# A two-layer decoder trunk: GpSimd sums of the down operand blocks, and down results placed in PSUM ahead of the tail's products

## What is computed

```python
h = rms_norm(x, ffn_pre_g[l])
f = jax.nn.silu(jnp.einsum('bsd,df->bsf', h, w_gate[l])) * jnp.einsum('bsd,df->bsf', h, w_up[l])
f = jnp.einsum('bsf,fd->bsd', f, w_down[l])
x = x + rms_norm(f, ffn_post_g[l])
# next layer
h = rms_norm(x, attn_pre_g[l]); u = h @ w_in[l]   # then four mixers, w_out, norm, residual
```

## Time and profile before

| | |
|---|---|
| three runs | 1068.89, 1071.06, 1071.44 us, median 1071.06 |
| the profiled execution | 1069.37 us, of which its span is 1067.6 |
| TensorE busy | 1028.0 us, 96% |
| VectorE busy | 896.6 us, 84% |
| ScalarE busy | 539.7 us, 51% |
| GpSimd busy | 65.2 us, 6% |
| mean granted TensorE clock | 0.993 |

### The profile page before, as it was taken

One profiled execution on the slowest core, in us unless ns is written; L12 is line 12 of the kernel. 1 busy time (PEld: TensorE's weight loads), 2 busy tenths in 40 slices (PEclk: granted clock), 3 DMA queues, 4 the chain that ended last, 5 costly groups with the idle time before them and its releaser, 6 DMA issues.

```text
span 1067.6 us, 21327 instructions
## 1 busy us (share of the span) xinstructions
PE 1028.0 (96%) x8470; PEld 832.6 (78%) x8470; DVE 896.6 (84%) x1788; ACT 539.7 (51%) x968; POOL 65.2 (6%) x86
## 2 busy tenths in 40 slices
PE   8999999999999998999988999999999999989996
PEld 5888895597888887888477888847878888878872
DVE  6999988985889899778699888988758989997657
ACT  5645454653666665426254363455446666654231
POOL 1000000010111110000000000000011111100000
PEclk9999999999999999999998999999999999999998
DMA  9512321363678863526034131224447777634212
GB/s 339 194 61 87 112 67 53 100 149 79 173 173 206 206 179 102 168 80 225 12 108 130 61 118 61 80 80 121 89 114 174 194 203 180 182 121 121 79 60 79
DMA packets 72883, 136.69 MB, mean 128 GB/s; under 512 B 8656, under 2 KB 8912, under 8 KB 72656
## 3 DMA queue, kind: packets, MB, share of 16 engines
q1 hardware_dynamic: 62992, 117.50, 33.6%
q0 software_dynamic: 9792, 17.83, 10.8%
HBM read 133.20 MB, written 2.10 MB: 127 GB/s over the span
## 4 chain that ended last, share of the span: by engine, by line
PE 72%; DVE 16%; issue 5%; ACT 4%; SPq 1%; DMA 1%; DVEq 0%; ACTq 0%
PE ps L696 31%; PE ps L804 17%; PE ps L873 14%; DVE ring L1660 4%; PE ps L700 3%; PE ps L894 2%; PE ps L1025 1%; DVE R L2029 1%; PE ps L1009 1%; ACT ring L1095 1%; DVE gbc L2047 1%; DMA raw<-weights_dram 1%; DVE ps L2105 1%; DVE E L1774 1%; SPq L617 1%
## 5 line engine op out<-in xcount | busy, mean ns | idle before, releaser
L1660 DVE SCALAR_TENSOR_TENSOR ring<-raw,ring 128x512 f16<-128x512 f32 (+2 forms) x368 | 320.3, 901 | 61.4 <-ACT ring L1095 61.3
L1095 ACT ACTIVATE ring<-raw 128x512 f16<-128x512 f32 (+2 forms) x368 | 278.0, 796 | 137.0 <-DVE raw L1630 59.9
L696 PE MATMUL ps<-hT,ring 128*128 128x256 f16 (+1 forms) x1632 | 195.5, 279 | 0.0
L696 PEld LDWEIGHTS ps<-hT,ring 128*128 128x128 f16 x1632 | 159.4, 98 | 28.8
L804 PE MATMUL ps<-E,ring 128*128 128x256 f16 x1224 | 145.3, 273 | 10.5 <-ACT gt L1095 9.7
L804 PE MATMUL ps<-hT,ring 128*128 128x256 f16 x1224 | 145.4, 273 | 0.0
L804 PEld LDWEIGHTS ps<-E,ring 128*128 128x128 f16 x1224 | 118.1, 98 | 29.5 <-ACT gt L1095 14.7
L696 PE MATMUL ps<-ring,hT 128*128 128x256 f16 x1152 | 134.6, 274 | 3.6 <-DVE hT L1782 3.5
L804 PEld LDWEIGHTS ps<-hT,ring 128*128 128x128 f16 x1224 | 119.8, 98 | 13.8
L696 PEld LDWEIGHTS ps<-ring,hT 128*128 128x128 f16 x1152 | 112.7, 99 | 19.5 <-issue 4.4
L1822 DVE SCALAR_TENSOR_TENSOR E<-E,par 128x256 f32<-128x256 f32 x240 | 102.0, 476 | 0.2
(11 more groups left out here) (172 smaller groups left out, 1148.3 us busy)
## 6 DMA issues: line engine op xcount, KB each, us to landing
raw<-weights_dram SPq DMA_DIRECT2D x402, 256.0 KB, 3.5
raw<-weights_dram POOLq DMA_DIRECT2D x68, 256.0 KB, 5.1
gbc<-gains_dram SPq DMA_DIRECT2D x8, 512.0 KB, 5.6
xs<-x_dram SPq DMA_DIRECT2D x4, 512.0 KB, 6.5
U<-weights_dram SPq DMA_DIRECT2D x8, 256.0 KB, 7.4
out_dram<-xs SPq DMA_DIRECT2D x8, 256.0 KB, 2.0
cst<-consts_dram SPq DMA_DIRECT2D x1, 1296.0 KB, 11.9
bd<-pool_w_dram SPq DMA_DIRECT2D x8, 16.0 KB, 9.7
```

Source lines behind the costliest of these rows:

```text
L696: ins = mm(dst, st, mv_, start=first and i == 0, stop=last and i == 2, **kw)
L1095: return A(dst, src, ACT.Copy, scale=scale)
L1660: V.scalar_tensor_tensor(out=at[1], in0=src, scalar=W_SCALE, in1=at[0], op0=ALU.mult, op1=ALU.subtract).then_inc(lo_split, 1)
```

## The change

1. `fS_sums` moves to GpSimd, as four instructions with no scalar_tensor_tensor among them. In GpSimd's queue it stands ahead of the accumulating DMAs of block 2p+5 (the last one behind those of block 21).
2. On ScalarE the hi halves of these sums (`fS_hi`) stand behind both shared results' copies, `u_copy` and `v_copy`, and ahead of weight chunks 2 and 3; on VectorE `fS_lo` stands behind `c22_add`. The order of chunks in the units f = 20 and 21 is changed too.
3. For tiles 1 to 3 `yq` is put into the tile's banks ahead of its tail products, which accumulate on it: `y0_copy` on ScalarE and `y1_sum` on VectorE. Only tile 0 keeps `y_sum`. `square_y` of tiles 1 to 3 waits for the unit alone. Two matmuls for each layer are added in `dn_seven`, which write half banks that ScalarE then overwrites.
4. Around the step to the second layer the splits of slots 2, 3 and 4 and the squares, norms and halves are put in another order, and three numbers of AT change.

```diff
-        ("pre_T", 2): 39, ("pre_T", 3): 63, ("moba_T", 0): 65, ("moba_T", 1): 82, ("moba_stage", 0): 106,
+        ("pre_T", 2): 33, ("pre_T", 3): 56, ("moba_T", 0): 70, ("moba_T", 1): 82, ("moba_stage", 0): 106,
...
+            def fS_sums(l, p):
+                i = 4 * (fS_no(l, p) - 1)
+                pool.wait_ge(f_sb, fno(l, 2 * p + 1, 0))
+                if i:
+                    pool.wait_ge(s_lo, 2 * (fS_no(l, p) - 1))
+                nc.gpsimd.tensor_tensor(f_sum[:, 0:2 * HALF].rearrange("p (c t) -> p c t", c=2),
+                                f_all[:, HALF:3 * HALF].rearrange("p (c t) -> p c t", c=2),
+                                f_all[:, 3 * HALF:4 * HALF].unsqueeze(1).to_broadcast([P, 2, HALF]),
+                                ALU.subtract).then_inc(s_sum, 1)
+                nc.gpsimd.tensor_tensor(f_sum[:, 2 * HALF:3 * HALF], f_all[:, 3 * HALF:4 * HALF], f_all[:, HALF:2 * HALF],
+                                ALU.subtract).then_inc(s_sum, 1)
+                pool.wait_ge(s_sum, i + 2)
+                nc.gpsimd.tensor_tensor(f_sum[:, 2 * HALF:3 * HALF], f_sum[:, 2 * HALF:3 * HALF], f_all[:, 2 * HALF:3 * HALF],
+                                ALU.subtract).then_inc(s_sum, 1)
+                pool.wait_ge(s_sum, i + 3)
+                nc.gpsimd.tensor_tensor(f_sum[:, 3 * HALF:4 * HALF], f_sum[:, 2 * HALF:3 * HALF], f_all[:, 0:HALF],
+                                ALU.add).then_inc(s_sum, 1)
             for i, n in enumerate(FAST_SLOTS):
+                l, f = n // SLOTS, n % SLOTS - GU0
+                for p in DN_FAST:
+                    if f == 2 * p + 5:
+                        fS_sums(l, p)
...
+                        if first and g and blk == 6:
+                            mm(bank[banks[t]][:, half(1)], a[0][:, tok(t)], dn_blocks(n, j, 0, blk, blk + 1),
+                               start=False, stop=True, skip_group_check=True)
...
-                fresh = tail0 and p == PLAIN[0]
+                fresh = tail0 and p == PLAIN[0] and t == 0
+                if k == TAIL0 and t:
+                    pe.wait_ge(y1_in, (NT - 1) * l + t)
+                    pe.wait_ge(y0_in, 5 * l + 2 * t - 1)
...
+            def y0_copy(l, t):
+                act.wait_ge(q_sb, 6 * (2 * l + 2))
+                copy(bank[PAIR[t]][:, :], yq[t][:, 0:512]).then_inc(y0_in, 1)
+                if t > 1:
+                    act.wait_ge(y1_in, (NT - 1) * l + t)
+                    copy(bank[PAIR[t] + 1][:, half(1)], yq[t][:, 512 + HALF:DM]).then_inc(y0_in, 1)
...
+            def y1_sum(l, t):
+                dve.wait_ge(q_sb, 6 * (2 * l + 2))
+                cols = slice(0, 512 if t == 1 else HALF)
+                b = bank[PAIR[t] + 1][:, cols]
+                V.tensor_tensor(b, b, yq[t][:, 512:DM][:, cols], ALU.add).then_inc(y1_in, 1)
```

More of the change, by code:

```diff
@@ L1347, in main_steps @@
                     due = fp % 2 and in_seven(fp)
-                    if not due:
+                    late = due or f >= FT - 2
+                    if not late:
                         split_hi_chunks(new, 1, 2)
                     hidden_hi(l, *HIDDEN[i - 1])
+                    if f in FAST:
+                        u_copy(l, f)
+                    if late:
+                        split_hi_chunks(new, 1, 2)
+                    else:
+                        split_hi_chunks(new, 2, 3)
+                    if f in FAST:
+                        v_copy(l, f)
                     if due:
                         fS_hi(l, fp // 2)
[L1353 to L1359, removed]
+                    if f == FT - 1:
+                        break
+                    if late:
+                        split_hi_chunks(new, 2, 3)
                     split_hi_chunks(new, 3, 4)
                 silu(l, *HIDDEN[i1 - 1])
+                split_hi_chunks(FREED_BY[l * NU + FIRST_OF[GU0] + i1 - 2], 2, 4)
                 split_hi(*FREED_BY[l * NU + FIRST_OF[GU0] + i1 - 1])
@@ L1637, in split_lo_part, with lo_part @@
                     dn_weight_sums(slot, part // 2)
+                lo_part(slot, part)
+            def lo_part(slot, part):
+                n = PARTS * slot + part
                 if fast(slot) and part == 1:
@@ L1736, in norm_y @@
                 r = rstd(t, (y_sq, n + 1))
+                if between:
+                    between()
                 if t == 0:
@@ L2129, in main_steps @@
                     due = fp % 2 and in_seven(fp)
-                    if due:
-                        fS_sums(l, fp // 2)
-                    else:
+                    if not due and not down:
                         split_lo_chunks(new, 1, 2)
@@ L2136, in main_steps @@
                         c12_add(l, f)
+                    if down:
+                        for part in range(2):
+                            lo_part(new[0], part)
+                        if f == FT - 2:
+                            dn_weight_sums(new[0], 1)
+                            c22_add(l, f)
+                            fS_lo(l, fp // 2)
+                            for part in range(2, PARTS):
+                                lo_part(new[0], part)
+                        else:
+                            c22_add(l, f)
+                        continue
                     if due:
-                        fS_lo(l, fp // 2)
                         split_lo_chunks(new, 1, 2)
```

133 lines of the change are left out of this document (74 added, 59 removed).

## The result

| | before | after |
|---|---|---|
| median, us (range, 4 runs each) | 1069.97 (1068.24 to 1071.44) | 1080.96 (1079.33 to 1082.50) |
| span of the profiled execution | 1067.6 | 1079.3 |
| gate and up stage of a layer | 163.10 | 172.01, 171.99 |
| seven-product down stage of a layer | 78.54 | 78.76, 78.75 |
| from the first layer's tail to the second's gate and up stage | 286.04 | 282.41 |

The changed kernel is slower: ratio 1.0103, interval 1.008 to 1.0127. The stage lengths are differences of TensorE's rows at the stages' borders, such as 425.29 in the earlier trace rows and 1031.51 in the earlier trace rows.

A forecast was written before the change was run, and what follows sets the result against it. TensorE, busy for 96% of the span, was taken as the bound, so only its waits, half clock and end could give time. +6.3 - 4.9 - 6.7 - 2.2 + 0.4 = -7.1 us gave 1064 us, range 1047 to 1083.

The forecast's parts named there:

- Rival A: Gate and up: GpSimd's sums end late beside VectorE's SBUF reads, +1.4 us a pair, +20 us, 1084 us; chance 0.27.
- units 20 and 21: Last two gate and up units: they lose 0.8 us instead of 3.24, -4.9 us for two layers.
- the step: Step into the second layer: shorter waits and no half clock, partly lost at the first attention stages; -6.7 us.
- Even unit: Gate and up: `u_copy` no longer waits for the sums, so the 0.57 us lost in an even unit are gone.
- Odd unit: Gate and up: hidden comes late, the unit takes 10.19 us, the pair 19.36 against 18.91; +6.3 us over 14 pairs.
- GpSimd's sums: Gate and up: four instructions of 1280 columns in all, taken at 3.5 us, between 1.8 and 5.2.
- the cover of 0.8: Gate and up: sums end at 391.0, ScalarE asks at 391.8; each further us costs 14 us for the kernel.
- no half clock: Step into the second layer: TensorE would not run at half clock there, where it had cost 2.0 us less 1.6.
- End and added matmuls: After TensorE's last matmul the last square starts earlier, -2.2 us; four added matmuls of 256 columns cost 0.44 us.
- GpSimd's queue: Accumulating DMAs of slot 21 start behind the sums but stay hidden, unless the sums end after 393.3.
- Rival B: Gate and up: no wait moves and both units of a pair are free, 14.3 us less, 1048 us; chance 0.25.

The follow-up runs named there:

- E1: The changed kernel with the sums of the down operand blocks made by VectorE again, in three instructions behind hidden; 1066.54 us, ratio 0.9966.
- E3: The changed kernel with ScalarE's `fS_hi` moved behind chunk 2 of the weights in even units, GpSimd still making the sums; 1056.68 us, ratio 0.9874.
- E6: The changed kernel with GpSimd's first sum made twice in each pair; 1107.95 us, ratio 1.0361.
- E4: The kernel before with only the sums moved to GpSimd, `fS_hi` still ahead of `u_copy`; 1120.95 us, ratio 1.0471.
- E8: E2 with 96 GpSimd instructions that nobody waits for (adds and memsets) put into layer 1; 1075.78 us, ratio 1.0051.
- E5: The changed kernel with the edits of E1 and E3 together: sums on VectorE, halves behind chunk 2; 1052.46 us, ratio 0.9830.
- E2: The kernel before, with its gate and up loop and sums kept, plus the new tail, step and end; 1061.47 us, ratio 0.9922.
- E7: E3 with ScalarE's copy of the first attention transposes moved ahead of the eighth weight block's splits; 1057.51 us, ratio 0.9882.
- E9: E5 with E7's edit, and 13 of VectorE's 18 convolution taps moved behind the fourth attention maximum; 1055.42 us, ratio 0.9865.
- E10: The kernel before with only ScalarE's `fS_hi` moved behind `v_copy`; 1106.14 us, ratio 1.0338.

## Why the prediction was wrong

I forecast 1064 and got 1081: Rival A, priced at 1084, instead of the forecast. Rival A is right in its mechanism; that its number is so near is in part luck. Its own terms (391.0 and 2.6 us) give 393.6 and not the 393.2 that I wrote, so 1.8 us a pair and some 1089, and it left the other terms as forecast. The pair lost only 0.94 us by GpSimd; units 20 and 21 and the step, both too good in the forecast, made up for it. By steps, on the profile's scale:

- **Even unit: right.** 9.17 us, no wait, as walked.
- **Odd unit, apart from GpSimd: right.** The walk gave 19.36 us for a pair with the sums on time; E1, where they are on time (because VectorE makes them), shows 19.35, with waits of 0.45 and 0.21 us in the places forecast.
- **GpSimd's sums: the step that failed.** I took 3.5 us, and they take 5.2, past the cover of 0.8. The prediction priced that end at 0.9 us a pair; the rows show 0.94. Its 12.6 us would have made the sum +5.5; the rest to the measured +11.7 is 3.1 in units 20 and 21, 3.1 at the step, and small terms. E1, E3 and E6 show it from three sides: sums on time, the queue behind them freed, and the dose. What went wrong inside the step: 3.5 us was a good price for the four alone (0.72 us for 256 columns in E4's idle time and 1.26 for 512 give 3.4, and E8's shortest adds give the same), but I put it into the sum as if VectorE were idle beside them. The rival's mechanism should have been the forecast, since `hidden_lo`, the weight sums and the lo halves all read two operands from SBUF. The Trainium skill (SBUF — State Buffer, section "Who interferes with whom") says that exactly such an instruction contends with a GpSimd instruction that reads SBUF, and not with one that only writes, and that one with at most one SBUF input does not contend; E8 agrees in all three cases. That the other side is blocked for the whole instruction, as my prediction has it, the section says outright of VectorE's two-port modes only, beside its general word of an exclusive lock. The rows fit it: an add of 0.73 us took up to 1.84, 1.1 more, with instructions of 1.22 us beside it.
- **Not seen: what the sums do to VectorE.** I counted 1.6 us of work off it in each pair. It gets back 1.69: 0.53, 0.11, 0.52 and 0.53 on the four instructions shown above, against 0.68, 0.68, 1.22 and 0.68. E5 against E3 shows that the whole move is a loss even where GpSimd is not waited for.
- **Units 20 and 21: sign right, size wrong.** Forecast 19.14 us for the two, measured 20.69 (before 21.58): -1.8 us in two layers for -4.9. With the sums on VectorE they take 19.99 (E1) and 19.97 (E5), so in each layer GpSimd has 0.7 of the miss and my walk 0.8.
- **The step: right in mechanism, too large.** -6.7 forecast, -3.6 measured. The same code gives -6.4 in E1 and -5.25 in E2, where a norm late in the step is waited for 1.2 us longer. The limit that I named, VectorE's maxima, is the right one (E7 and E9), and so is its time: 578.4, the earliest start that I gave for the next stage, is 74.6 us into the tail, and the transposes stand at 74.3 in E2 and 74.9 in E1. Two things that the sum has at nothing made the changed kernel 2.7 us worse than E1. A weight split at the tail's start waited 1.77 us for its DMA, so the sums of the down results ended 5.3 us into the tail, not 3.8 (tile 0's operand is waited for 1.76 us, in E1 and E2 0.3): 1.4 us. And I wrote "no half clock"; ScalarE's copy behind a split was late, and 42 matmuls behind that wait took 5.72 us for 4.75 and four transposes 0.88 for 0.47: 1.4 us.
- **End and added matmuls: right.** -2.2 and +0.4 us.
- **GpSimd's queue: right.** The accumulating DMAs stayed hidden; no engine waits for one in unit 19. (By its own numbers, 399.0 less 5.1, the limit was 393.9, not 393.3.)
- **Rival B** (no wait moves) is what E5 has in its pairs, by another order than it was argued for.

E5's step (282.68) is 3.0 us longer than E1's with the same code there. The rows tell why. E1, then E5:

```profile
568.26 0.63 PE L704 MATMUL ps<-cst,U 128*128 128x128 f32 x4 [3.29 <-ACT U L1105]
568.73 4.75 PE L700 MATMUL ps<-ring,hT 128*128 128x256 f16 x42
```

```profile
562.02 1.09 PE L704 MATMUL ps<-cst,U 128*128 128x128 f32 x4 [3.91 <-ACT U L1105]
562.90 6.74 PE L700 MATMUL ps<-ring,hT 128*128 128x256 f16 x42
```

The wait is 0.6 us longer, because the splits ahead of the copy waited longer for their weights. Behind it the granted clock is 0.50 until 566.9 (in E1 it is 1.00), which costs 2.0 us on the 42 matmuls and 0.4 on the transposes. What stays open is when the clock falls: at the step it did with waits of 3.91 us (E5), 3.26 (E8), 3.18 (after), 3.12 (E3) and 2.78 (E7), and did not with 3.29 (E1), 2.73 (E6) and 2.44 (E2), and no run varies this alone.

## What to carry to other kernels

Before work is moved to GpSimd, list what VectorE does in the same microseconds. Each instruction of it with two operands in SBUF can pay for GpSimd's reads, and GpSimd pays too, so the move can cost more than the work was (here 1.69 us on VectorE for 1.53 taken off it). And put an instruction that waits for a slow helper last in its engine's queue before its reader, on every engine that it passes: E3 gained 24 us by one place on ScalarE, E10 lost 37 where VectorE's place had been left out.

## What was unexpected of the hardware

- A GpSimd add of 128x256 took 0.73 to 1.84 us beside VectorE's work; a memset of that size took 0.31 to 0.314 in all 32.
- GpSimd's work that nobody waits for made the program 14.3 us slower (E8 against E2), with 39.8 us of large adds beside a VectorE that the others depend on.
- Two kernels with the same code and waits of 3.29 and 3.91 us in the same place differ by 2.4 us in what follows, because only the second fell to the half clock (E1 and E5). Removing such a wait only moved the half clock to the next one (E7).
